# Spatial gating products of a hybrid decoder step on one core: one float32 product against three rounded ones at another place in TensorE's queue

## The reference, cut to what matters

```python
def chunk_spatial_gate(u, v, w_s, b_s):
    vc = v.reshape(n, t_pad // CHUNK, CHUNK, h, dh)
    mask = jnp.tril(jnp.ones((CHUNK, CHUNK), dtype=bool))
    ws = jnp.where(mask[None], w_s, jnp.zeros_like(w_s))
    mixed = jnp.einsum('hij,ncjhd->ncihd', ws, vc) + b_s.T[:, :, None]
    ...
    return u * mixed

h = rmsnorm(x, g_pre)
z = h @ w_in                                    # 1024 -> 2432
u, v, ga, xb, gb, q, gc = jnp.split(z, cuts, axis=-1)
vn = rmsnorm(v per head, g_v)
out_a = chunk_spatial_gate(u, vn, w_s, b_s) * silu(ga)
xc = causal_conv(xb); r, i = sigmoid(blockwise xc @ w_a + b_a), sigmoid(blockwise xc @ w_x + b_x)
hs = scan(exp(log_a(r)), sqrt(-expm1(2 log_a)) * i * xc)      # h = a h + x over the positions
out_b = hs * silu(gb)
out_c = cross_attend(q, mk, mv) * silu(gc)
y = x + rmsnorm(concat(out_a, out_b, out_c) @ w_out, g_post)
```

## Time and profile before

| | |
|---|---|
| median of three runs | 377.1 us (377.0 to 377.11) |
| profiled execution | 376.63 us |
| its span, first to last instruction | 374.9 us |
| TensorE busy | 367.4 us, 98% |
| VectorE busy | 284.0 us, 76% |
| ScalarE busy | 214.5 us, 57% |
| GpSimd busy | 145.3 us, 39% |
| chain that ended last, by engine | PE 88%, DVE 6%, ACT 2%, issue 2%, DMA 1% |
| granted TensorE clock, mean | 0.998 of full speed |

### The profile page before, as it was taken

One profiled execution on the slowest core, in us unless ns is written; L12 is line 12 of the kernel. 1 busy time (PEld: TensorE's weight loads), 2 busy tenths in 40 slices (PEclk: granted clock), 3 DMA queues, 4 the chain that ended last, 5 costly groups with the idle time before them and its releaser, 6 DMA issues.

```text
span 374.9 us, 5746 instructions
## 1 busy us (share of the span) xinstructions
PE 367.4 (98%) x2274; PEld 349.4 (93%) x2274; DVE 284.0 (76%) x362; ACT 214.5 (57%) x371; POOL 145.3 (39%) x86
## 2 busy tenths in 40 slices
PE   8999999999999999999999999999999999999993
PEld 8999889999999999999999899999998899988873
DVE  4998897524668977867758999696399969359596
ACT  6986826853553652674969815944947255203722
POOL 3021771572454323742193065220551994002300
PEclk9999999999999999999999999999999999999999
DMA  7995035611130143424211001703122033030632
GB/s 288 393 400 232 0 125 104 224 58 56 59 111 2 56 121 104 126 93 131 58 58 34 24 7 52 281 22 143 62 52 118 2 112 114 1 116 33 194 114 113
DMA packets 18939, 41.14 MB, mean 110 GB/s; under 512 B 4408, under 2 KB 8800, under 8 KB 18656
## 3 DMA queue, kind: packets, MB, share of 16 engines
q1 hardware_dynamic: 18768, 40.70, 31.9%
q10 hardware_dynamic: 144, 0.08, 0.1%
HBM read 35.90 MB, written 4.87 MB: 109 GB/s over the span
## 4 chain that ended last, share of the span: by engine, by line
PE 88%; DVE 6%; ACT 2%; issue 2%; DMA 1%; DVEq 0%; SPq 0%; ACTq 0%
PE ps L481 54%; PE ps L750 12%; PE ps L768 6%; PE ps L558 3%; PE ps L618 2%; PE ps L694 1%; PE ps L607 1%; PE ps L586 1%; DMA mixT<-in_xT 1%; PE ps L588 1%; PE ps L608 1%; DVE mixT L1542 1%; PE ps L668 1%; PE ps L715 1%; PE ps L642 1%
## 5 line engine op out<-in xcount | busy, mean ns | idle before, releaser
L481 PE MATMUL ps<-x_hi,w_hi 128*128 128x344 f32 x450 | 145.4, 323 | 0.0
L481 PE MATMUL ps<-x_lo,w_hi 128*128 128x344 f32 x450 | 143.7, 319 | 0.0
L481 PE MATMUL ps<-x_hi,w_lo 128*128 128x344 f32 x450 | 143.7, 319 | 0.0
L481 PEld LDWEIGHTS ps<-x_hi,w_hi 128*128 128x128 f32 x450 | 84.6, 188 | 0.2
L481 PEld LDWEIGHTS ps<-x_lo,w_hi 128*128 128x128 f32 x450 | 84.5, 188 | 0.2
L481 PEld LDWEIGHTS ps<-x_hi,w_lo 128*128 128x128 f32 x450 | 84.6, 188 | 0.0
L1226 POOL TENSOR_TENSOR w_lo<-w_stage,w_hi 128x1024 fp32r<-128x1024 f32 x17 | 43.1, 2540 | 98.3 <-ACT w_hi L838 83.9
L1368 DVE TENSOR_TENSOR zT<-ps,rstdB 128x344 f32<-128x344 f32 x33 | 16.7, 510 | 20.1 <-PE ps L481 19.9
L838 ACT ACTIVATE w_hi<-w_stage 128x1024 fp32r<-128x1024 f32 x17 | 17.8, 1053 | 21.0 <-PE ps L481 21.0
L1334 POOL TENSOR_TENSOR zT<-zT,x_ring 128x1024 f32<-128x1024 f32 x4 | 12.9, 3214 | 36.6 <-DVE zT L1801 36.6
L750 PE MATMUL ps<-x_hi,w_hi 128*128 128x512 f32 x64 | 25.5, 398 | 0.0
(11 more groups left out here) (338 smaller groups left out, 839.2 us busy)
## 6 DMA issues: line engine op xcount, KB each, us to landing
w_stage<-in_w_tiles SPq DMA_DIRECT2D x17, 512.0 KB, 4.0
mixT<-in_xT SPq DMA_DIRECT2D x8, 516.0 KB, 8.2
x_ring<-in_x_all SPq DMA_DIRECT2D x6, 512.0 KB, 4.3
o_y<-zT SPq DMA_DIRECT2D x5, 512.0 KB, 2.9
zT<-in_w_mem SPq DMA_DIRECT2D x4, 512.0 KB, 11.8
cache<-in_kc SPq DMA_DIRECT2D x8, 256.0 KB, 4.0
cache<-in_vcT SPq DMA_DIRECT2D x8, 256.0 KB, 3.2
spread<-p_rows SPq DMA_DIRECT2D x16, 128.0 KB, 3.1
```

Of the source, the lines that this page charges most:

```text
L481: last = pe.matmul(ps[:, bank, 0:GN], w[:, slot, wk], xx[:, k, cols], start=(x == 0 and n == 0), stop=(x == KT - 1 and n == 2))
```

## The change

The rounded high halves of the masked weights (`ws_hi`) and of the v rows (`v_hi`) are copies on ScalarE, the low halves (`ws_lo`, `v_lo`) subtractions on VectorE; they lie in space of `sc_r` (which shares its memory with `cache` and `spread`) and of `zT_r`. Each spatial product becomes three matmuls. TensorE's order, the banks and the waits are changed, VectorE's order of `mixed`, `low_xc(1)`, `evac` and `scan(0)` too, and SyncE's w_out loads wait for the last spatial product.

```diff
-SPATIAL_BANKS = (6, 7, 4, 5, 3, 4, 6, 7)
+SPATIAL_BANKS = (6, 7, 4, 3, 6, 7, 3, 4)
...
+        flat_r = sc_r[:, :, :].rearrange("p a b -> p (a b)")
+        v_hi = flat_r[:, 0:NCH * AW].rearrange("p (c n) -> p c n", c=NCH)
+        ws_hi = flat_r[:, 6 * 512:7 * 512].rearrange("p (h n) -> p h n", h=AH)
+        ws_lo = flat_r[:, 7 * 512:8 * 512].rearrange("p (h n) -> p h n", h=AH)
+        v_lo = zT_r[:, :, :].rearrange("p a b -> p (a b)")[:, TT:TT + NCH * AW].rearrange("p (c n) -> p c n", c=NCH)
...
@@ SyncE @@
             load_w(18, 0)
             sp.wait_ge(vsum_s_done, NS)
+            sp.wait_ge(sp_done, 2 * AH)
...
@@ TensorE, gates @@
-                    if 7 <= n <= 10:
-                        pe.wait_ge(mix_done, n - 4)
+                    if n == 10 or n == 12:
+                        pe.wait_ge(mix_done, 3 if n == 10 else 7)
...
@@ TensorE, spatial @@
-                pe.wait_ge(vn_done, i // AH + 1)
+                pe.wait_ge(vtoklo_done, i // AH + 2)
                 if i < 2:
                     pe.wait_ge(vt_used, 9)
                 elif i < 4:
-                    pe.wait_ge(gate_used, 6)
-                elif i < 6:
-                    pe.wait_ge(gate_used, i + 3)
+                    pe.wait_ge(gate_used, (8, 10)[i - 2])
                 else:
-                    pe.wait_ge(mix_done, i - 5)
-                pe.matmul(ps[:, SPATIAL_BANKS[i], 0:AW].rearrange("p (c n) -> p c n", c=4), wsT[:, h, :],
-                          v_tok[:, c0:c0 + 4, h * AD:(h + 1) * AD], start=True, stop=True).then_inc(sp_done, 1)
-
-            pe.wait_ge(w_masked, 1)
-            for q in range(4):
-                gemm(14 + q // 3, q % 3, q // 3)
-                if q % 2 == 0:
-                    for i in range(2 * q, 2 * q + 4):
-                        spatial(i)
-                if q > 0:
-                    gates(1, q - 1)
+                    pe.wait_ge(mix_done, (1, 2, 4, 4)[i - 4])
+                if i == 7:
+                    pe.wait_ge(gate_used, 11)
+                out = ps[:, SPATIAL_BANKS[i], 0:AW].rearrange("p (c n) -> p c n", c=4)
+                hi, lo = v_hi[:, c0:c0 + 4, h * AD:(h + 1) * AD], v_lo[:, c0:c0 + 4, h * AD:(h + 1) * AD]
+                pe.matmul(out, ws_hi[:, h, :], hi, start=True, stop=False)
+                pe.matmul(out, ws_hi[:, h, :], lo, start=False, stop=False)
+                pe.matmul(out, ws_lo[:, h, :], hi, start=False, stop=True).then_inc(sp_done, 1)
+
+            gemm(14, 0, 0)
+            gemm(14, 1, 0)
+            gemm(14, 2, 0)
+            gates(1, 0)
+            gates(1, 1)
+            for i in range(4):
+                spatial(i)
+            gemm(15, 0, 1)
+            gates(1, 2)
+            for i in range(4, 8):
+                spatial(i)
 
             for g in range(NG):
                 gemm(15 + (g + 1) // 3, (g + 1) % 3, 1 - (g + 1) // 3)
                 for c in range(3 * g, 3 * g + 3):
-                    pe.wait_ge(mix_done, 9)
+                    pe.wait_ge(mix_done, (5, 6, 8)[c] if c < 3 else 9)
...
@@ ScalarE @@
             split_xc(1)
+            act.wait_ge(vsum_s_done, NS)
+            act.wait_ge(w_masked, 1)
+            act.activation(ws_hi, wsT[:, :, :], ACT.Copy).then_inc(vtokhi_done, 1)
             split_tile(15)
+
+            def v_high(q):
+                act.wait_ge(vn_done, q + 1)
+                act.activation(v_hi[:, 4 * q:4 * q + 4, :], v_tok[:, 4 * q:4 * q + 4, :], ACT.Copy).then_inc(vtokhi_done, 1)
+
+            v_high(0)
             root_b(0)
             gate_sigmoids(1, 0)
             gate_sigmoids(1, 1)
+            v_high(1)
             place(0)
             split_tile(16)
             gate_sigmoids(1, 2)
...
@@ VectorE @@
             rest(0)
+
+            def v_low(q):
+                part = slice(4 * q, 4 * q + 4)
+                dve.wait_ge(vtokhi_done, q + 2)
+                dve.tensor_tensor(v_lo[:, part, :], v_tok[:, part, :], v_hi[:, part, :].bitcast(F),
+                                  ALU.subtract).then_inc(vtoklo_done, 1)
+
             strip_lows(strips[1], ((lead, second, 2), (tail, third, 0)), 5)
-            mixed(0)
-            mixed(1)
             dve.wait_ge(rest_done, 1)
             low_xc(1)
-            mixed(2)
-            mixed(3)
+            evac(14, 0, zT[:, 9, grp(0)])
+            dve.wait_ge(vtokhi_done, 1)
+            dve.tensor_tensor(ws_lo, wsT[:, :, :], ws_hi.bitcast(F), ALU.subtract).then_inc(vtoklo_done, 1)
+            v_low(0)
             times_factor(1)
+            evac(14, 1, zT[:, 9, grp(1)])
+            evac(14, 2, zT[:, 9, grp(2)])
+            for i in range(4):
+                mixed(i)
+            v_low(1)
             times_factor(2)
-            evac(14, 0, zT[:, 9, grp(0)])
-            evac(14, 1, zT[:, 9, grp(1)])
-            mixed(4)
-            mixed(5)
             scan(0)
-            mixed(6)
-            mixed(7)
-            evac(14, 2, zT[:, 9, grp(2)])
+            for i in range(4, 8):
+                mixed(i)
             mixed_samples()
```

More of the change, by code:

```diff
@@ L312, in build @@
             "yf_ready", "xf_in"))
-        vsq_done, vsum_done, vroot_done, vr_done, vn_done = map(sem, (
-            "vsq_done", "vsum_done", "vroot_done", "vr_done", "vn_done"))
+        vsq_done, vsum_done, vroot_done, vr_done, vn_done, vtokhi_done, vtoklo_done = map(sem, (
+            "vsq_done", "vsum_done", "vroot_done", "vr_done", "vn_done", "vtokhi_done", "vtoklo_done"))
         ga_done, gar_done = map(sem, ("ga_done", "gar_done"))
```

## The result

The changed kernel takes 382.5 us in the median (382.25 to 382.9, four runs) against 377.11 us (377.0 to 377.13): 1.0147 times the time of before, 95% interval 1.0134 to 1.0159, 5.4 us slower. The forecast was 381.0, range 378.4 to 383.3. The profiled execution took 382.9 us, 6.3 over the profiled one of before; about 0.9 of that is chance between the two, since before's lies 0.5 under its median and this one 0.4 over its own.

The account below looks back on a forecast made before the run. The prediction took TensorE, busy 98% and executing in order, as the bound. Cheaper products -0.96, waits +0.95 and +3.9 gave +3.9 us on the 377.1 median: 381.0 us, range 378.4 to 383.3.

Parts of the forecast that it names:

- TensorE full, so every wait counts: TensorE, busy 98% with an in-order queue, has no later wait to shrink, so any added wait moves everything behind it.
- Price of the products: Spatial products on TensorE: three rounded matmuls take 0.525 us against 0.645 in float32; eight products save 0.96 us.
- First stall: TensorE at spatial 0 waits about 0.95 us for VectorE's v_low(0), due 221.82, starting 222.8.
- The turns: VectorE's ws_lo and v_low(0) alternate by whole instructions with GpSimd's, standing still 4.5 us (2.1 and 2.4).
- Second stall: TensorE at spatial 7 waits 3.9 us for ScalarE's sigmoid n = 10, queued behind place(0), which waits for late scan(0).
- A, the forecast: +3.9 us: Both waits at the spatial products occur, less cheaper matmuls: tile 15 group 1 starts 3.9 us later, 381.0 us; chance 0.62.
- rival C: After the wait at spatial 7, idle TensorE runs four microseconds at half clock, losing 2.0: +5.9, 383.0 us; chance 0.13.
- Rival B: VectorE and GpSimd don't block one another: scan(0) at 226.75, spatial 7 at 233.25, +1.4, 378.5 us; chance 0.12.
- D: The scan's chain is in time, both TensorE waits vanish and 0.96 us of cheaper matmuls stay: 376.1 us; chance 0.06.
- What rides along: Added ScalarE copies, later SyncE loads and mixed_samples ending near 241 are hidden and add no stall; unhidden copies, 3.7 us.

Follow-up runs that it names:

- the kernel with both edits: Changed kernel with ScalarE's gate_sigmoids(1,2) ahead of place(0), and GpSimd's low_w(15), then keep_xc(0), behind v_low(0): 376.41 us, 0.9978 times before.

## Why the prediction was right, and where it was not

- **TensorE full, so every wait counts.** Right: the lag of 6.0 us at the end of the stretch is carried unchanged through 120 matmuls and more.
- **Price of the products.** 0.525 forecast, 0.528 measured. The other price that the prediction named, a saving of a quarter (1.29 us), is too much; 0.94 is what the timeline has. The pause in the projection takes 0.2 of it, which nothing in the trace of before showed.
- **First stall.** Forecast 0.95, measured 0.75. The turns came as worked out. TensorE was 0.73 late in this execution, and so was VectorE when it began `low_xc(1)` (215.11 for 214.38); at the end of `v_low(0)` it was only 0.43 late (223.18 for 222.75), since `ws_lo`, `low_w(15)` and `v_low(0)` together took 0.3 less than reckoned.
- **Second stall.** Forecast 3.9, measured 3.72, through the very chain described: scan 229.69 (229.2), copy 233.53 (233.0), sigmoid 235.55 (235.15), spatial 7 at 236.22 (235.74). Each is some 0.5 late, which is what was left of the late start at `v_low(0)`; TensorE arrived 0.7 late, so the stall was 0.2 shorter. Moving the sigmoids confirmed it.
- **The step that failed.** The sum of "A, the forecast: +3.9 us" has no term for the clock: it took TensorE for full speed behind the stall, and kept the other case as rival C, at 0.13. C is what happened, A's stalls and a slow stretch behind them. C's price was 2.0 us, taken from the length of the warm-up at the kernel's start; it measured 1.56, which is twelve matmuls at 0.287 instead of 0.157 us. With it the sum is 3.9 + 1.56 = 5.5 against 5.4 measured. The forecast of 381.0 was 1.5 short, which is this term, and the measured 382.5 lies in the range only because that was drawn up to C.
- **What the trace of before had to say on it.** The prediction set the full digits of the earlier trace rows against C. A nine there is 90% or more of a slice of 9.4 us, and the mean granted clock was 0.998. The missing part lies at the end: TensorE's last matmul starts at 368.74, and some 4 us later its clock falls.

```profile
373.00:374.00 1.00, 0.00 (x0) 0.00 (x0) 0.00 (x0) 0.00 (x0) 0.00 (x0) 0.58 0.97 359
374.00:374.90 0.90, 0.00 (x0) 0.00 (x0) 0.00 (x0) 0.00 (x0) 0.00 (x0) 0.50 0.00 0
```

So that trace did show an idle array throttled. It gave no price, since no matmul follows, and the warm-up gave none for certain: the granted clock reads 1.00 in the microseconds 1 to 5, so that the half rate there was read from the length of the weight loads alone. The Trainium skill (TensorE: Matmul & The Clock Gate, HAM oscillation) warns that an array left idle between groups of matmuls is throttled and starts the next group slow; it was a better guide than the digits of the slices. The runs agree that it is throttled: the granted clock fell to 0.50 behind 3.56, 2.87 and 2.24 us of idle, and stayed at 1.00 behind 0.97 and 0.6. In none of the three did the next group start slow at once; the slow steps began 0.8 to 1.2 us behind the restart.
- **Rival B** fell by its rows: 2.69 and 3.96 us beside GpSimd, 0.68 and 1.75 without. Its places came true where GpSimd was put out of the way: `scan(0)` at 226.97 (226.75) and spatial 7 at 233.51 (233.25), and again its time, 378.5, lacked the clock: 380.35. **D** fell in the changed kernel, but its 0.96 is what the kernel with both edits gets, less the pause.
- **What rides along.** SyncE's later loads and `mixed_samples` near 241.4 delayed nobody, as forecast.

## What to carry to other kernels

Where one engine is full, price a change in another engine's queue by what stands behind it: here 3.9 us of subtractions on VectorE, an engine that is 76% busy, cost 5.4, because one sigmoid stood in line behind the scan that they delayed, and putting that sigmoid first, which needed nothing from the scan, gave 5.0 back. When a bank is reassigned, follow the engine that must empty it to everything ahead of it in its queue. And price a stall of TensorE twice, for its length and for the slow matmuls behind it: the stalls of 2.2 to 3.6 us here had 1.5 us or so of the second kind, those of 1 us and less had none.

## What the runs showed of the hardware that was not expected

- A wait of 2.24 us was enough for half clock. The fall came behind the restart, not in the gap: in the changed kernel the granted clock is 1.00 in every microsecond from 232 to 237, the first five matmuls behind the gap of 3.56 us are 0.25, 0.18, 0.18, 0.15 and 0.17 us apart, and the slow ones began 0.9 us after the restart (237.15 against 236.22).
- At the kernel's end, where no matmul follows, the moment of the fall differs between executions: by the windows of a microsecond it lies about 2 us behind the last matmul in the float32 kernel with the sigmoids first, 4 in the kernel before and 5 in the changed one. So one trace does not tell when the clock of an idle array will fall.
- TensorE's weight loads paused for 0.32 us with no visible cause in the kernels with rounded products, tens of microseconds behind the change.
- Profiled executions differ by up to 0.7 us in the first 180 us, where the kernels do the same: the transposes of v began at 182.4 in the changed kernel, at 181.7 in the kernel before and between these in the others. Differences of some tenths can't be read from one profile.
